# Modulation units of the first attention on GpSimd, low output one head later, next queries behind an exponential

## The reference

```
mod_lat = split((silu(c) @ w_mod[l] + b_mod[l]), 6)
mod_ctx = split((silu(c_ctx) @ w_mod[l] + b_mod[l]), 6)
a_lat = rms_norm(x, g1) * (1 + mod_lat[1]) + mod_lat[0]      # the same for the context
m_lat, m_ctx = token_mixers(a_lat, a_ctx)                    # attention | retention | Fourier, then w_out
x = x + mod_lat[2] * m_lat
x = x + mod_lat[5] * (square(relu(modulate(x, 3, 4) @ w_ff1)) @ w_ff2)
```

## Time and profile before

| | us |
|---|---|
| median of the runs | 1704.47 (1702.3 to 1705.03) |
| the profiled execution | 1702.21 |
| its span on the core | 1700.4 |
| PE busy | 1606.9 (94%) |
| DVE busy | 1042.7 (61%) |
| ACT busy | 588.5 (35%) |
| POOL busy | 584.6 (34%) |

### The profile page before, as it was taken

The page is one execution under the profiler, slowest core; times in us unless marked ns, Lnnn a source line. Parts: engine busy times, 40 slices in busy tenths (PEclk is TensorE's granted clock), DMA queues, the critical chain, the costliest instruction groups (busy, mean ns, idle before and its releaser), DMA issues.

```text
span 1700.4 us, 23038 instructions
## 1 busy us (share of the span) xinstructions
PE 1606.9 (94%) x8800; PEld 1365.0 (80%) x8800; DVE 1042.7 (61%) x1481; ACT 588.5 (35%) x951; POOL 584.6 (34%) x324
## 2 busy tenths in 40 slices
PE   6899989989999999999899988998999799999998
PEld 2788878978888888888788887887897688888887
DVE  5778966868765767566466776585544544444442
ACT  4522435652532221211212345234662432332321
POOL 1336661012333222233222443336003444444442
PEclk9899999989999999999999999999999899999999
DMA  9333111105333434344343432231002132333332
GB/s 325 101 126 118 51 44 50 51 9 154 94 99 116 120 112 131 99 142 133 91 143 103 129 110 75 71 91 38 1 1 82 55 99 88 97 95 90 99 99 87
DMA packets 168653, 162.33 MB, mean 95 GB/s; under 512 B 6624, under 2 KB 132208, under 8 KB 168560
## 3 DMA queue, kind: packets, MB, share of 16 engines
q1 hardware_dynamic: 168560, 161.02, 31.1%
HBM read 158.90 MB, written 2.10 MB: 95 GB/s over the span
## 4 chain that ended last, share of the span: by engine, by line
PE 57%; issue 25%; DVE 7%; POOL 4%; ACT 4%; DMA 1%; SPq 1%; POOLq 0%; DVEq 0%; ACTq 0%
PE psA L1931 17%; PE psB L1931 16%; POOL Wlo L525 4%; PE psA L1711 2%; PE psA L1712 2%; PE psA L1713 2%; PE psB L1711 2%; PE psB L1713 2%; PE psB L1712 2%; PE ps L1903 2%; DVE Ab L1438 1%; PE psS L1713 1%; PE psS L1712 1%; PE psS L1711 1%; PE psS L1572 1%
## 5 line engine op out<-in xcount | busy, mean ns | idle before, releaser
L525 POOL TENSOR_TENSOR Wlo<-raw,Whi 128x1024 fp32r<-128x1024 f32 x158 | 384.5, 2434 | 829.8 <-ACT Whi L663 829.8
L663 ACT ACTIVATE Whi<-raw 128x1024 fp32r<-128x1024 f32 x181 | 191.4, 1059 | 635.0 <-PE psB L1931 269.4
L1438 DVE TENSOR_TENSOR Ab<-Tb 128x512 f32<-128x512 f32 (+2 forms) x68 | 167.9, 2469 | 175.9 <-ACT Tb L929 175.8
L1931 PE MATMUL psA<-Ahi,Whi 128*128 128x512 f32 (+1 forms) x432 | 138.1, 362 | 11.4 <-issue 5.0
L1931 PE MATMUL psB<-Ahi,Whi 128*128 128x512 f32 (+1 forms) x424 | 135.1, 362 | 2.6 <-POOL Wlo L529 2.2
L1931 PE MATMUL psA<-Ahi,Wlo 128*128 128x512 f32 (+1 forms) x432 | 137.5, 361 | 0.0
L1931 PE MATMUL psA<-Alo,Whi 128*128 128x512 f32 (+1 forms) x432 | 136.8, 359 | 0.0
L1931 PE MATMUL psB<-Ahi,Wlo 128*128 128x512 f32 (+1 forms) x424 | 134.9, 361 | 0.0
L1211 DVE SCALAR_TENSOR_TENSOR X<-psB,modT,X 128x256 f32<-128x256 f32 (+1 forms) x104 | 67.1, 664 | 109.7 <-PE psB L1931 109.6
L1931 PE MATMUL psB<-Alo,Whi 128*128 128x512 f32 (+1 forms) x424 | 134.3, 359 | 0.0
L1931 PE MATMUL psA<-Hhi,Whi 128*128 128x512 f32 (+1 forms) x368 | 117.7, 362 | 14.1 <-DVE X L1211 12.8
(11 more groups left out here) (331 smaller groups left out, 3525.9 us busy)
## 6 DMA issues: line engine op xcount, KB each, us to landing
raw<-in_w_ff_dram SPq DMA_DIRECT2D x135, 512.0 KB, 4.1
modraw<-in_w_mod_dram SPq DMA_DIRECT2D x72, 512.0 KB, 4.3
raw<-in_w_in_dram SPq DMA_DIRECT2D x36, 512.0 KB, 3.7
modst<-in_w_mod_dram SPq DMA_DIRECT2D x16, 512.0 KB, 5.8
raw<-in_w_out_dram SPq DMA_DIRECT2D x16, 512.0 KB, 4.3
modat<-in_w_mod_dram SPq DMA_DIRECT2D x8, 512.0 KB, 3.8
macc<-in_w_ff_dram SPq DMA_DIRECT2D x5, 512.0 KB, 3.5
modraw<-in_dft_lat_dram SPq DMA_DIRECT2D x8, 257.0 KB, 3.6
```

Of the source, the lines that this page charges most:

```text
L525: nc.gpsimd.tensor_tensor(Wlo[:, s, :], raw[:, s, :], Whi[:, s, :], ALU.subtract).then_inc(S["lo_done"], 1)
L663: nc.scalar.activation(whis[slot], raws[slot], ACT.Copy).then_inc(S["hi_done"], 1)
L1438: V.tensor_tensor(Ab[:, k % 2, c0:c1], Tb[:, k % 2, c0:c1], Tb[:, k % 2, c0:c1], ALU.mult).then_inc(S["h_full"], 1)
L1931: last = mm(dst[:, c0:c1], wt, x[:, i, c0:c1], start=f, stop=e)
```

## The change

Three edits in the code of the attention.

1. The eight units go from VectorE to GpSimd. `mid` on VectorE and its call are gone. GpSimd has a `mid(i)` for a whole unit, which it runs for all eight between its last gating in layer 0 and `low_stash`. One product covers both streams: the slice of weights is repeated over the streams and `csil` along the 512 columns. The second product goes to `macc` and is added to the sum, since GpSimd has no multiply-and-add here: 3 operations for the first unit of a chunk, 4 for the others, 30 in all, each of 128x1024, each waiting for the one before. A wait for `sc_ready` stands ahead of them.
2. The low output of block b goes from step 8b+12 to 8b+13 on VectorE, behind the maximum of that step, in both layers; only the last block of a layer keeps its step.
3. `query_hi` on ScalarE goes from ahead of the exponential of head 5 to behind that of head 4, in both layers.

```diff
+        def mid(i):
+
+            src, acc, part, wd, w = modat[:, i % NSA, :], matt[:, i // 4], i % 4, 20 + i, MID + i - MOD0
+            pool.wait_ge(modat_in[i % NSA], 16 * (i // NSA + 1))
+            if i:
+                pool.wait_ge(S["mod_used"], w)
+            x = [src[:, kk * MCH:(kk + 1) * MCH].unsqueeze(1).to_broadcast([P, 2, MCH]) for kk in range(2)]
+            col = [csil[:, 2 * part + kk, :].unsqueeze(2).to_broadcast([P, 2, MCH]) for kk in range(2)]
+            steps[1] += 1
+            nc.gpsimd.tensor_tensor(acc if part == 0 else macc[:, :, :], x[0], col[0], ALU.mult).then_inc(S["mid_step"], 1)
+            pool.wait_ge(S["mid_step"], steps[1])
+            if part:
+                steps[1] += 1
+                nc.gpsimd.tensor_tensor(acc, acc, macc[:, :, :], ALU.add).then_inc(S["mid_step"], 1)
+                pool.wait_ge(S["mid_step"], steps[1])
+            nc.gpsimd.tensor_tensor(macc[:, :, :], x[1], col[1], ALU.mult).then_inc(S["mod_step"], 3)
+            pool.wait_ge(S["mod_step"], wd * 3 + 3)
+            nc.gpsimd.tensor_tensor(acc, acc, macc[:, :, :], ALU.add).then_inc(S["mod_used"], 1)
...
             if l == 0:
+                pool.wait_ge(S["sc_ready"], NT)
+                for i in range(8):
+                    mid(i)
                 for i in range(STASH):
                     low_stash(i)
...
-                    if k == 5 and b + 1 < TT[l]:
-                        query_hi(b + 1)
...
+                    if k == 4 and b + 1 < TT[l]:
+                        query_hi(b + 1)
...
-                if l == 0 and 10 <= s < 42:
-                    mid(s - 10)
...
-                if s >= 12 and (s - 12) % 8 == 0 and (s - 12) // 8 < TT[l]:
-                    b = (s - 12) // 8
+                at = 12 if s == n_items + 4 else 13
+                if s >= at and (s - at) % 8 == 0 and (s - at) // 8 < TT[l]:
+                    b = (s - at) // 8
                     dve.wait_ge(S["aoT_hi"], l * NT + b + 1)
```

More of the change, by code:

```diff
@@ L157, in build @@
     tokbank = [psA[:, 0:512], psA[:, 512:1024], psB[:, 0:512], psB[:, 512:1024], psS[:, 0:512], psS[:, 512:1024]]
-    names = """consts_in late_in xa_in xb_in row_copied row_turned tmp_in stored rows_T par_ready csil_ready mod_pe mod_first mod_used mod_step modp_ready mod_red mod_evac xT_ready x_ready
+    names = """consts_in late_in xa_in xb_in mid_step row_copied row_turned tmp_in stored rows_T par_ready csil_ready mod_pe mod_first mod_used mod_step modp_ready mod_red mod_evac xT_ready x_ready
         stat_sq stat_done sq_sum rt_sqrt rstd_ready rb_ready dve a_full a_hi a_lo_even a_lo_odd hi_done lo_done unit_done proj_ready p_ready qk_var qk_sqrt
@@ L529, in low_part @@
             nc.gpsimd.tensor_tensor(Wlo[:, u % 2, :], raw[:, u % 2, :], Whi[:, u % 2, :], ALU.subtract).then_inc(S["lo_done"], 1)
-        steps = [0]
+        steps = [0, 0]
         def rotate(v, t, ready, out_sem):
```

## The result

The kernel after takes 1694.5 us (median of 5 runs, 1692.84 to 1696.29) against 1704.47 before (1702.3 to 1705.03): the ratio is 0.9945, 95% interval 0.993 to 0.9959, so 10 us less, 7 to 12 by the interval. The profiled execution of after took 1695.64 (span 1693.9, mean granted clock 0.980), 6.6 less than the 1702.21 before.

A forecast was written before the change was run, and what follows sets the result against it. TensorE was taken to bound the kernel, except where it waits for VectorE in the first attention's context items. The terms 6.3 - 0.4 - 1.0 + 0 + 0.2 = 5.1 us took 1704.47 to 1699.4, range 1695.5 to 1705.6.

The forecast's parts named there:

- Context items: Items 33 to 47 of the first attention: 25.28 us become 19.0, a gain of 6.3, bounds 3.3 to 7.5.
- Block 3: Items 29 to 33, first attention: freed VectorE time and GpSimd waits nearly cancel, +0.2 us, between -2.5 and +1.2.
- the waits take as much if GpSimd still runs: Block 3, first attention: VectorE's waits for GpSimd cancel a gain of up to 1.2 us.
- Block 0: First attention, 4-tile steps: three VectorE operations wait for GpSimd, -1.0 us, between 0 and -2.5; query copies cost extra.
- Blocks 1 and 2: First attention, 5-tile steps: slack of 1.8 us hides VectorE's waits for GpSimd, 0, down to -2.0 together.
- Second layer: Second attention: TensorE is full, so the low output's move gives nothing; the query copies' early place costs 0.2 us.
- The profiled execution lies 2.3 below the median: Whole kernel: before's profiled 1702.21 against its median 1704.47; after's 1697.1 was likewise set against 1699.4.
- The gain is not given back: Behind the first attention: everything waits relative to its end and keeps TensorE full, so the gain stays.
- The clock falls all the same: Rival, context items: the clock falls as before, some five steps cost 1.70 for 1.05, time 1702.4; chance 0.24.
- The lock eats it: Rival, blocks 0 to 3: each VectorE wait is nearly a whole GpSimd piece, time 1705.6; chance 0.12.
- The bias operation takes the lock: Rival, some 30 items: VectorE's one-element bias operation also waits 1.2 us for GpSimd, time 1709.1; chance 0.08.
- Nothing moves: Rival, context items: another engine's chain bounds them, so the time stays 1704.5; chance 0.06.

The follow-up runs named there:

- e6: After with GpSimd's unit operations cut to 8 of 512 columns, the rest of the two gate chunks left out: 1694.23 us, ratio 0.9948 to before.
- e7: After with nothing on GpSimd: the 32 operations stay on VectorE, in steps 3 to 31 instead of 10 to 41; 1694.71 us, ratio 0.995 to before.
- e5: After with GpSimd starting its units only once ten items are done, so it works beside the context items: 1697.36 us, ratio 0.9976 to before.
- e4: After with the query copies back ahead of the exponential of head 5: 1700.84 us, 12 runs from 1694.05 to 1708.02, ratio 0.9987 to before.
- e1: After with both reorderings undone, only the units on GpSimd: 1696.63 us, 12 runs from 1694.25 to 1710.01, ratio 0.9984 to before.
- after, again: The kernel after once more, with no edit: 1692.9 us (1690.41 to 1695.64), ratio 0.9936 to before.
- e4, again: One more execution, for a second trace, of after with the query copies back ahead of the exponential of head 5: 1706.7 us.
- e8: After with GpSimd's unit operations cut to 8 of 512 columns and the query copies back ahead of head 5's exponential: 1692.59 us, ratio 0.9951 to before.
- e2: After with the units back on VectorE, only the two reorderings kept: 1697.16 us, ratio 0.9976 to before.
- e3: After with the low output back in its old step, all else kept: 1698.92 us, ratio 0.9986 to before.
- before, again: The kernel before once more, one execution with no edit, for a second trace: 1705.54 us, on a chip where its other runs have a median of 1701.31.

## Where the prediction held, and where it was too small

**Context items, 6.3 forecast, 6.76 measured.** 25.28 became 18.52, and by pieces: items 33 to 36 took 3.83 (4.0 forecast), 36 to 41 took 7.84 (7.1), 41 to 47 took 6.85 (7.4), and the 0.5 for the softmax sums was not needed. The mechanism and its size hold. The 1.85 us of copies on ScalarE were there as the sum had them, as the 1.42 us stall above; what the sum left out is that the clock can fall behind it. In after it did, and that is the 0.7 by which items 36 to 41 passed the forecast; e6 and e7, with the stall and no fall, take 7.05 there, the forecast's 7.1.

**Block 3, 0.2 forecast, 1.20 measured.** Items 28 to 33 went from 11.06 to 9.86, the whole of the upper bound. The step that failed is "the waits take as much if GpSimd still runs". In after GpSimd ended at 334.56, and the subtractions of this block stand at 335.70 and 337.99, both 0.69 long. GpSimd's 70 us were forecast from products of 2.08; they took 1.90, so it ran 68.5 us, and the bound 333 to 349 was right only at its early edge. But the early end is not what decides: in e5 GpSimd runs through the whole block and the items take 9.86 all the same. Its subtractions took 0.69 and 0.70, started 0.10 and 0.24 ahead of a GpSimd operation, and the waits of the biases and sinks (1.22 for 0.17) and of the denominators (0.31 for 0.17) were hidden. The price that was set against the gain did not arise in either kernel.

**Block 0, -1.2 forecast with the copies, -0.20 measured.** The waits came as described: 0.61, 1.08, 0.72 and 1.47 us beyond the lengths of 0.69 and 0.17, on average 0.97 where 1.2 was forecast. Items 5 to 9 took 8.27 for 8.07. The step that failed is the -1.0: waits of this size were taken to add up beyond a slack of 1.0 and stall TensorE, and in these items of after TensorE waits for VectorE not once. In e6, without the lock, the same items take 8.11, so the lock's own price there is 0.16. That VectorE makes up the lateness between the waits fits, but no run isolates it; and in e4 the slack was passed.

**Blocks 1 and 2, 0 forecast, -0.01 measured** (46.94 for 46.93). The eight operations with two SBUF inputs waited 0 to 0.50 there, 0.3 on average, so 1.2 was too much as a mean. **Second layer, -0.2 forecast, -0.07 measured** (its items 0 to 31 took 76.80 for 76.73).

In the first attention the forecast was 6.3 - 1.2 + 0 + 0.2 = 5.3; with 0.5 more in the context items, 1.0 in block 3, 1.0 in block 0 and 0.06 in items 0 to 5 it is 7.8. So the mechanism held, and two terms of the sum, both prices of the lock, were set at 1.0 each where it cost 0.16 and nothing.

**"The profiled execution lies 2.3 below the median"** was carried over to after as a constant, and it is none: after's profiled execution lies 1.1 above its median, and 1702.21 stands among the 35 runs of before on the chip of e1 to e4, 0.4 above their median of 1701.8, and not among the five with the median of 1704.47. 7.8 from the attention alone would make 1704.5 - 7.8 = 1696.7, inside the range. (By its own sum, 1704.5 - 8.7, the range would begin at 1695.8 and not 1695.5.) What took the time out of the range is the other 2.2 outside the attention, which the sum put at nothing. Its cause stays open. It need not be scatter: on another chip after, again is 9.95 lower than before by the medians (8 to 13 by the interval of its ratio). One candidate is a fall of the clock near 465 us, worth 1.5 us, which the last section shows; but in the profiled pair the rest is 1.3 longer in after, so these traces don't show the 2.2.

**Rivals.** *The clock falls all the same*: it did, but for 4 us instead of 9, and items 36 to 47 took 14.69 where the forecast without a fall had 14.5. That it was short in after, and absent in e6 and e7 behind the same stall, no row of before foretold. *The lock eats it*: not in after, whose 11 runs are all low, but with the query copies elsewhere (e4) 7 of 12 runs are above 1700, and in e4, again items 9 to 28 lost 9.8, where blocks 1 and 2 were to lose 2.0 at most. "Deterministic once GpSimd restarts right behind each" was wrong: VectorE 0.06 us behind a GpSimd start took 2.86 (e4), 0.10 ahead of one 0.69 (e5). *The bias operation takes the lock*: it is 0.21 or 0.22 long in every row beside GpSimd, here and in e4 and e5; the rival falls. The rule of the Trainium skill, Advanced Engine Details and Errata, "VectorE Performance Modes", that was set beside it agrees with these rows. *Nothing moves* fell with the result.

**"The gain is not given back"** holds for the waits: TensorE's wait behind the attention is 2.23 us in after and 2.25 in before. The copies' early place was costed at 0.4. e6 and e8 differ in it alone: in items 5 to 28 it costs nothing (55.04 for 55.01), in the second layer 0.3 (76.86 for 76.54, where 0.2 was forecast; after and e4 differ there by 0.08). What the sum did not see is its worth: with it the subtractions start where no GpSimd sum holds them for its whole length. e1, which has the copies late too, had two runs in 12 above 1707; that these are the same event fits, but e1's one trace shows 0.41 us of it (a subtraction of 2.85) and the clock at 1.00.

## What to carry to other kernels

Work that has slack in long steps goes beside long steps: here it was enough, with the two reorderings, that 32 operations end before most of the short steps, on either engine. Work on GpSimd has a second price, paid by whatever VectorE operation with two SBUF inputs starts just behind it; cost it as one whole GpSimd operation at the worst place, and ask whether the stall that follows can bring the clock down. When a term hangs on which of two operations starts first, a mean is no forecast: give it as a range with its worst case, and read from a trace whether TensorE waits at all.

## What the runs showed of the hardware

**A short stall can cost a multiple of itself through the clock.** In e4 the windows at 276 and 285 show it: 1.7 us of idle TensorE, then 14 us at 0.50; in e4, again it is 2.45 us, then 0.50 from 304 to 314. The same stall does not always do so: 1.42 us in block 4 is followed by 0.57 in after and by 1.00 in e6 and e7.

**The same wait far behind the change, with and without a fall.** Both kernels wait some 2.2 us for GpSimd's low weights behind the attention. TensorE's timeline of before:

```profile
466.54 0.79 PE L1931 MATMUL psB<-Ahi,Whi 128*128 128x512 f32 x1 [2.25 <-POOL Wlo L529]
```

A window of before around it:

```profile
464.00:475.00 11.00, 8.75 (x35) 6.97 (x34) 8.98 (x11) 3.73 (x7) 4.73 (x2) 0.84 0.21 52
```

TensorE's timeline of after:

```profile
460.93 0.50 PE L1945 MATMUL psB<-Ahi,Whi 128*128 128x512 f32 x1 [2.23 <-POOL Wlo L529]
```

The same window of after:

```profile
464.00:475.00 11.00, 11.00 (x61) 9.45 (x60) 8.83 (x12) 2.69 (x4) 3.90 (x2) 1.00 0.34 101
```

Before, the clock falls behind it (0.84 in the mean of the window), and the work behind it is 1.55 us later for it than in after. In the 14 profiled executions it fell in the seven whose item 47 starts after 362 us (both befores, e2, e3, e5 and both e4) and in none of the seven in which it starts before 360. So a kernel that is some microseconds sooner there gained 1.5 us more in these traces; why the one falls and the other doesn't was not tried, nor how often it is so in the timed runs. Against it stands a fall near 405 us, worth 1.8, that before has not and after and before, again have (it comes between 400 and 415).

**The rest of the scatter stays open.** Of the 3.4 us between the two executions of before, 1.8 is that fall; the remainder gathers between 600 and 940 us with no wait of its own, in both directions, as a pace some 2% different for some 50 us at a time. Differences of 3 us between single profiled executions of this kernel say nothing. The pieces of the attention repeat to 0.1 in before and in after, but not where the clock falls in some executions: e4's items 5 to 9 took 10.36 and 9.10, and items 0 to 5 took 15.88 and 14.87.
